# A hybrid decoder step on one core: where the convolution, its gate and the key norms of the gated DeltaNet heads are computed

## What is computed

```
conv = full[:, 0:T] * conv_w[0]
for j in range(1, G_CONV):                       # G_CONV = 4
    conv = conv + full[:, j:j + T] * conv_w[j]
q, k, v = split(silu(conv), 3)
q = l2norm(heads(q)) * HEAD_DIM ** -0.5
k = l2norm(heads(k))
beta = sigmoid(b_logit);  g = -exp(a_log) * softplus(a_logit + dt_bias)
G = cumsum(g);  decay = exp(G_i - G_j)           # inside chunks
```

## Time and profile before

| | us |
|---|---|
| median of 3 runs | 2923.39 |
| the profiled execution | 2920.07 |
| its span | 2917.9 |
| PE busy in the span | 2698.5 |
| DVE busy | 1668.2 |
| ACT busy | 947.1 |
| POOL busy | 161.5 |

### The profile page before, as it was taken

One profiled execution on the slowest core, in us unless ns is written; L12 is line 12 of the kernel. 1 busy time (PEld: TensorE's weight loads), 2 busy tenths in 40 slices (PEclk: granted clock), 3 DMA queues, 4 the chain that ended last, 5 costly groups with the idle time before them and its releaser, 6 DMA issues.

```text
span 2917.9 us, 59294 instructions
## 1 busy us (share of the span) xinstructions
PE 2698.5 (92%) x23238; PEld 2519.8 (86%) x23238; DVE 1668.2 (57%) x2503; ACT 947.1 (32%) x1694; POOL 161.5 (6%) x168
## 2 busy tenths in 40 slices
PE   8999999978887899999999999999787879999996
PEld 8999999857665789999999999988666668999996
DVE  5666337654646466663356653467456655666534
ACT  4333224332212243332233332333222223333323
POOL 1030110000000010001100001100000001000011
PEclk9999999977867999999999999999777889999998
DMA  4852334200000323222222222431000022222221
GB/s 110 106 90 88 88 93 135 59 24 5 10 8 2 94 74 90 87 87 83 79 87 86 86 83 87 130 99 39 27 1 9 10 65 59 80 86 86 88 88 56
DMA packets 380501, 201.67 MB, mean 69 GB/s; under 512 B 41461, under 2 KB 376821, under 8 KB 379528
## 3 DMA queue, kind: packets, MB, share of 16 engines
q1 hardware_dynamic: 377928, 197.46, 23.2%
q0 software_dynamic: 2400, 1.82, 1.9%
HBM read 188.07 MB, written 13.34 MB: 69 GB/s over the span
## 4 chain that ended last, share of the span: by engine, by line
PE 78%; DVE 10%; issue 5%; ACT 4%; DMA 1%; SPq 1%; DVEq 0%; POOLq 0%; ACTq 0%; POOL 0%
PE ps L683 53%; PE ps L738 24%; DVE ar L1926 3%; DVE ar L1920 2%; ACT ar L1421 2%; DVE wl L1804 1%; ACT wh L1352 1%; PE ps L1012 1%; SPq L530 1%; DVE x L1920 1%; DMA raws<-in_ffn_w_in 0%; DVE ar L1956 0%; DVE xl L1911 0%; DVE ar L1923 0%; DMA raws<-in_w_in 0%
## 5 line engine op out<-in xcount | busy, mean ns | idle before, releaser
L1804 DVE TENSOR_TENSOR wl<-raws,wh 128x1024 fp32r<-128x1024 f32 x336 | 411.3, 1225 | 662.0 <-ACT wh L1352 657.8
L683 PE MATMUL ps<-xh,wh 128*128 128x272 f32 x2880 | 604.8, 291 | 18.5 <-DVE wl L1804 16.0
L738 PE MATMUL ps<-ar 64*64 64x64 f32 (+13 forms) x5408 | 484.1, 277 | 133.7 <-ACT ar L1421 37.8
L683 PE MATMUL ps<-xh,wl 128*128 128x272 f32 x2880 | 599.8, 290 | 0.0
L683 PE MATMUL ps<-xl,wh 128*128 128x272 f32 x2880 | 598.5, 289 | 0.0
L738 PEld LDWEIGHTS ps<-ar 64*64 64x64 f32 (+6 forms) x5408 | 359.7, 162 | 233.1 <-issue 66.1
L1352 ACT ACTIVATE wh<-raws 128x1024 fp32r<-128x1024 f32 x336 | 355.1, 1058 | 407.1 <-PE ps L683 376.4
L683 PEld LDWEIGHTS ps<-xh,wh 128*128 128x128 f32 x2880 | 457.5, 190 | 21.6 <-DVE wl L1804 18.0
L683 PEld LDWEIGHTS ps<-xl,wh 128*128 128x128 f32 x2880 | 457.9, 190 | 0.0
L683 PEld LDWEIGHTS ps<-xh,wl 128*128 128x128 f32 x2880 | 457.4, 190 | 0.0
L683 PE MATMUL ps<-hh,wh 128*128 128x272 f32 x1408 | 292.2, 289 | 0.0
(11 more groups left out here) (190 smaller groups left out, 2724.0 us busy)
## 6 DMA issues: line engine op xcount, KB each, us to landing
raws<-in_ffn_w_in SPq DMA_DIRECT2D x176, 512.0 KB, 3.6
raws<-in_ffn_w_out SPq DMA_DIRECT2D x64, 512.0 KB, 4.0
raws<-in_w_in SPq DMA_DIRECT2D x42, 512.0 KB, 3.5
raws<-in_ffn_w_out SPq DMA_DIRECT2D x32, 384.0 KB, 3.4
raws<-in_w_out SPq DMA_DIRECT2D x16, 448.0 KB, 4.0
x_kept<-x SPq DMA_DIRECT2D x2, 2176.0 KB, 10.1
x<-x_kept SPq DMA_DIRECT2D x2, 2176.0 KB, 7.9
ar<-in_consts SPq DMA_DIRECT2D x2, 1337.5 KB, 6.6
```

The costliest lines, as they stand in the source:

```text
L683: ins = pe.matmul(ps[:, bank + h, 0:n1 - h * NH], w[u % 2][:, k, :], a[:, k0 + k, h * NH:n1], start=(first and k == 0 and n == 0), stop=(l ...
L738: return pe.matmul(dst, lhsT, rhs, start=start, stop=stop, **kw)
L1804: dve.tensor_tensor(wl[u % 2][:, :, :], raw[u % 2][:, :, :], wh[u % 2][:, :, :].bitcast(F32), ALU.subtract).then_inc(sem("wl_done"), 1)
```

## The change

The four taps and the silu of pairs 2 and 3 leave `prepare_gdn` of DVE and go to GpSimd, which does them in the first two periods. [...] The results stay in unused chunks of `xh` and `xl` (`over_x`), the scratch in chunks of `proj` that are no longer read. ACT's tanh of the pairs stand in the inverse of pair 0 and the preparation of pair 1, its squares in the inverse of pair 1. The gated DeltaNet preparations shrink to 26 steps: sums of squares first, then the roots (ACT copies the sums out of PSUM first), the Newton step on SBUF operands, beta, `cum`, and `dif` behind the first product steps of the recurrence; `token_major` is step 5.

```diff
-PREPARE_STEPS = (27, 27 + GATE_STEPS, 30, 30)
+PREPARE_STEPS = (27, 27 + GATE_STEPS, 26, 26)
...
+        over_x = sb("over_x", [P, 2, KC, NX])
...
+                if self.gd:
+                    self.W = [over_x[:, t, k, 0:NT] for t, k in (((0, 1), (1, 1), (0, 6)), ((1, 6), (0, 7), (1, 7)))[self.c]]
+                    self.sq = proj[:, GCH + self.c:GCH + self.c + 3:2, :]
+                    self.y = proj[:, self.c:self.c + 3:2, :]
...
+        conv_tmp = [over_x[:, 0, 0, 0:NT], over_x[:, 1, 0, 0:NT], proj[:, V_CH, :]]
+        tap_tmp = [pairs[3].W, [proj[:, GCH + 2 * j, :] for j in range(3)]]
+        CONVOLVED = lambda c, k: 45 * c + 36 + 2 * (k + 1)
```

PE, `prepare_gdn`, up to `token_major`, after:

```diff
+                    norm_sums_of(p)
+                    yield
+                    pe.wait_ge(sem("qk_out"), at(lay, "qk_out", c + 1))
+                    pe.wait_ge(sem("beta"), at(lay, "beta", 1))
+                    for h in range(2):
+                        ins = mm(ps[:, 2 + h, 0:NH], cst("sel", 8)[:, c * P:(c + 1) * P], proj[0:8, BA_CH, h * NH:(h + 1) * NH])
+                    ins.then_inc(*tick("beta_b"))
                     pe.wait_ge(sem("ge"), at(lay, "ge", c + 1))
...
                     ins.then_inc(*tick("cum"))
-                    for i in range(TILES):
...
-                    ins.then_inc(*tick("dif"))
-                    yield
                     yield
                     pe.wait_ge(sem("dec"), at(lay, "dec", 2 * q - 1))
...
                     yield
+                    pe.wait_ge(sem("kk_read"), at(lay, "kk_read", q + 1))
+                    for i in range(TILES):
...
+                    ins.then_inc(*tick("dif"))
                     yield
                     yield
                     pe.wait_ge(sem("dec"), at(lay, "dec", 2 * q))
                     pe.wait_ge(sem("dif_min"), at(lay, "dif_min", 3 * (c + 1)))
-                    pe.wait_ge(sem("qk_sq"), at(lay, "qk_sq", 2 * (c + 1)))
-                    blk_sum(U[:, 3, :], 0, "qk_sum")
-                    blk_sum(U[:, 4, :], 2, "qk_sum")
```

ACT:

```diff
+                def conv_tanh(p, k):
+                    act.wait_ge(sem("conv"), at(lay, "conv", CONVOLVED(p.c, k)))
+                    if p.c:
+                        act.wait_ge(sem("conv_s"), at(lay, "conv_s", k + 1))
+                    go(conv_tmp[k], p.W[k], ACT.Tanh, scale=0.5).then_inc(*tick("conv_t"))
...
+                def norm_roots(p):
+                    act.wait_ge(sem("qk_sum"), at(lay, "qk_sum", p.c + 1))
+                    act.wait_ge(sem("conv_s"), at(lay, "conv_s", 3 * (p.c + 1)))
+                    sums = ps[:, 3, 0:2 * NSAMP].rearrange("p (k n) -> p k n", k=2)
+                    go(p.sq[:, :, 0:SEQ], ps[:, 1:3, :])
+                    go(p.sq[:, :, SEQ:NT], sums)
+                    go(p.y[:, :, SEQ:NT], sums, ACT.Ln, bias=eps_l2).then_inc(*tick("a_ln"))
+                    go(p.y[:, :, 0:SEQ], ps[:, 1:3, :], ACT.Ln, bias=eps_l2).then_inc(*tick("qk_out"))
...
+                    go(p.y, p.y, ACT.Exp, scale=-0.5).then_inc(*tick("rs_exp"))
...
+                    if q == 1:
+                        for k in range(3):
+                            conv_tanh(pairs[3], k)
...
+                        if q == 0 and li == 1:
+                            for k in range(3):
+                                conv_tanh(pairs[2], k)
+                        if q == 1 and li == 2:
+                            act.wait_ge(sem("conv"), at(lay, "conv", 2 * 42 + 3))
+                            qk_squares(pairs[2])
+                        if q == 1 and li == 3:
+                            qk_squares(pairs[3])
```

DVE, `prepare_gdn`, after (the four calls of `tap`, the three silu operations and the later Newton step are gone from it):

```diff
+                    newton(p.y, p.sq, L2_EPS, p.sq, "rs_exp", "d_seq", q + 1)
+                    stt(U[:, K_, :], p.W[1], 0.5, p.y[:, 1, :], ALU.mult, ALU.mult).then_inc(*tick("d_seq"))
+                    dve.wait_ge(sem("beta_b"), at(lay, "beta_b", c + 1))
+                    stt(halves(U[:, BV, :]), halves(p.W[2]), 0.5, bank2(2), ALU.mult, ALU.mult).then_inc(*tick("d_seq"))
+                    dve.wait_ge(sem("d_seq"), last(lay, "d_seq"))
+                    stt(halves(U[:, NBK, :]), halves(U[:, K_, :]), -1.0, bank2(2), ALU.mult, ALU.mult).then_inc(*tick("kk_read"))
+                    stt(U[:, Q_, :], p.W[0], 0.5 * HD ** -0.5, p.y[:, 0, :], ALU.mult, ALU.mult).then_inc(*tick("d_seq"))
```

GpSimd, new, in front of its wait for `head_l` 4:

```diff
+                def tap(p, s):
+                    for j in range(3):
+                        ch = 2 * j + p.c
+                        wt = par("conv_w")[:, (3 - s) * 6 + ch:(3 - s) * 6 + ch + 1]
+                        dst = tap_tmp[p.c][j] if s else p.W[j]
+                        pool.tensor_scalar(dst[:, s:SEQ], proj[:, GCH + ch, 0:SEQ - s], wt, None, ALU.mult).then_inc(*tick("conv"))
+                        pool.tensor_scalar(by_samples(dst), xe[:, ch, :, 3 - s:7 - s], wt, None, ALU.mult).then_inc(*tick("conv"))
+                    conv_done()
+                    for j in range(3 if s else 0):
+                        dst, add = p.W[j], tap_tmp[p.c][j]
+                        pool.tensor_tensor(dst[:, s:SEQ], dst[:, s:SEQ], add[:, s:SEQ], ALU.add).then_inc(*tick("conv"))
+                        pool.tensor_tensor(dst[:, SEQ:NT], dst[:, SEQ:NT], add[:, SEQ:NT], ALU.add).then_inc(*tick("conv"))
...
+                        pool.tensor_tensor(conv_tmp[j], conv_tmp[j], p.W[j], ALU.mult).then_inc(*tick("conv"))
+                    conv_done()
+                    for j in range(3):
+                        pool.tensor_tensor(p.W[j], p.W[j], conv_tmp[j], ALU.add).then_inc(*tick("conv_s"))
...
+                pool.wait_ge(sem("xe"), at(lay, "xe", 1))
+                pool.sem_inc(passed, 1)
+                for s in range(4):
+                    tap(pairs[2], s)
...
+                for s in range(4):
+                    tap(pairs[3], s)
+                    if s == 1:
+                        conv_silu(pairs[2])
+                conv_silu(pairs[3])
```

More of the change, by code:

```diff
@@ L908, in banks_free, with norm_sums_of @@
                         pe.sem_inc(passed, 1)
+                def norm_sums_of(p):
+                    pe.wait_ge(sem("qk_sq"), at(lay, "qk_sq", 2 * (p.c + 1)))
+                    pe.sem_inc(passed, 1)
+                    for k in range(2):
+                        mm(ps[:, 1 + k, :], cst("blk"), p.sq[:, k, 0:SEQ])
+                    for k in range(2):
+                        ins = mm(ps[:, 3, k * NSAMP:(k + 1) * NSAMP], cst("blk"), p.sq[:, k, SEQ:NT])
+                    ins.then_inc(*tick("qk_sum"))
                 def prepare_rwkv(p):
@@ L983, in prepare_gdn @@
                     yield
+                    pe.wait_ge(sem("kk_read"), at(lay, "kk_read", q + 1))
+                    for i in range(TILES):
+                        for hp in range(2):
+                            g = ge[:, i, hp * HD:hp * HD + 1].broadcast_to([P, P])
+                            dst = ps[:, 2 + i // 2, (i % 2 * 2 + hp) * P:(i % 2 * 2 + hp + 1) * P]
+                            mm(dst, g, cst("gd")[:, 0:P], stop=False)
+                            ins = mm(dst, cst("neg_incl"), g, start=False)
+                    ins.then_inc(*tick("dif"))
                     yield
@@ L1582, in prepare_gdn @@
                     act.wait_ge(sem("state_out"), at(lay, "state_out", 64 * (q - 1)))
+                    norm_roots(p)
+                    yield
                     yield
@@ L1586, in prepare_gdn @@
                        ps[:, 0:2, :].rearrange("p a n -> p (a n)").rearrange("p (i k n) -> p k i n", i=TILES, k=2), ACT.Exp).then_inc(*tick("dec"))
-                    for n in range(2):
-                        act.wait_ge(sem("dif_min"), at(lay, "dif_min", 3 * c + n + 1))
-                        go(gram[:, 4 * n:4 * n + 4, 2 * P:3 * P], gram[:, 4 * n:4 * n + 4, 2 * P:3 * P], ACT.Exp).then_inc(*tick("dif_e"))
                     yield
@@ L1640, in inverse @@
                     yield
-                    for _ in range(1, len(LEVELS)):
+                    for li in range(1, len(LEVELS)):
+                        if q == 0 and li == 1:
[6 more added lines that the diff above has]
+                            qk_squares(pairs[3])
                         yield
@@ L2206, in prepare_gdn @@
                     dve.sem_inc(*tick("ge"))
-                    dve.wait_ge(sem("xe"), at(lay, "xe", 1))
-                    for k in range(3):
-                        tap(k)
-                        dve.wait_ge(sem("d_seq"), last(lay, "d_seq"))
+                    newton(p.y, p.sq, L2_EPS, p.sq, "rs_exp", "d_seq", q + 1)
+                    stt(U[:, K_, :], p.W[1], 0.5, p.y[:, 1, :], ALU.mult, ALU.mult).then_inc(*tick("d_seq"))
+                    dve.wait_ge(sem("beta_b"), at(lay, "beta_b", c + 1))
```

134 lines of the change are left out of this document (54 added, 80 removed).

## The result

The changed kernel took 2874.53 us in the median of its runs beside 2924.65 for the kernel before: a ratio of 0.984, 95% interval 0.9805 to 0.9875. Two later comparisons of the same two kernels gave 0.9838 (0.9811 to 0.9864) and 0.983 (0.9799 to 0.986). Its profiled execution took 2875.93 us, with a span of 2874.1 against 2917.9.

A forecast was written before the change was run, and what follows sets the result against it. PE was taken as the bound, busy 2698.5 of 2917.9 us. Gain -32.8 plus cover 21 gave -11.8: 2908.3 from the profiled 2920.07, 2911.6 from the median; forecast's own range 2901 to 2921, overall range 2885 to 2940.

The forecast's parts named there:

- The holes: Third and fourth periods up to token_major's first transposes: 24.4 and 23.0 us, instead of 35.9 and 34.4.
- The two moved finish steps: Finish steps pushed behind token_major in the third and fourth periods: charged 4.3 and 2.2 us.
- The gain: Third and fourth periods, shorter holes less moved finish steps: net 7.2 and 9.2 us, 16.4 a layer, 32.8 in all.
- rival (a): First two periods: cover nearly free, DVE seldom meets POOL, 2898; with PE's clock rising earlier, 2890; chance 0.24.
- The cover: Work added in the first two periods, mainly POOL slowing DVE: cost 10.5 us a layer, 21 in all.
- The price of a meeting: First two periods: a two-input SBUF operation of DVE loses 0.5 us to POOL's operations.
- my sign: Expected in the changed profile: DVE's two-input operations between 620 and 700 above 1.1 us, where they were 0.72.
- POOL's prices: First two periods: tensor_scalar 0.96 us, add 1.36, contention 15; POOL done at 699, before ACT asks at 706.6.
- rival (c): Second period: ACT waits for POOL's late taps; decides above 1.25 us per tensor_scalar; 2936 or 2955 us; chance 0.17.

The follow-up runs named there:

- e5_conv_only_delay: Kernel before with only convolution and silu moved to the first two periods, plus six idle DVE operations in each hole: 2921.73 us, 1.0014 to the kernel before.
- e1_cover: Kernel before plus POOL's and ACT's added work of the first two periods as idle work that nothing reads: 2922.28 us, ratio 1.0009.
- part one alone: Kernel before with convolution and silu moved to the first two periods, norms left late with 30 steps: 2921.95 us, ratio 1.0014.

## Why the prediction was wrong

**The holes: right.** 23.5 and 22.1 us stand against my 24.4 and 23.0. The chain went as I wrote it down; ACT's part of it in the fourth period:

```profile
875.50 1.14 ACT L1436 ACTIVATE ar<-ps 128x1024 f32<-128x1024 f32 x2 [1.00 <-DVE xl L1960]
...
880.62 1.11 ACT L1436 ACTIVATE ar<-ar 128x1088 f32<-128x1088 f32 x1
```

From the head's end at 875.2 to the end of the exponential are 6.5 us; I had 6.3. DVE's Newton step ended at 10.5 for my 10.3.

**The two moved finish steps: about right.** Charged 4.3 and 2.2; the second layer's rest of the third period grew by 5.4 (57.9 to 63.3) and the fourth's by 1.4 (42.8 to 44.2). With four more steps the third period only shifts this work, as I assumed, but the fourth loses 4.3 us, which I had not seen.

**The gain: mis-sized, because PE's clock was put at nothing.** "Net 7.2 and 9.2 us" took the rest as the same but for the moved steps. Measured are 14.5 and 5.8 in the third periods and 10.9 and 11.0 in the fourth, 42 in all for my 33. The first layer had 65.3 us at 0.74 in its rest (I cited that row, and used it only in rival (a), as 8 us); after the change it is 63.2 or 63.3 at 0.86 or 0.87, in both layers and in all three profiles of the changed kernel. Over the four periods of both layers the matmuls took 10 to 19 us less for a term that my sum does not have. Why the clock comes so is open; e5_conv_only_delay shows that it hangs on the hole before.

**The cover: the step that failed.** "Cost 10.5 a layer, 21 in all" measured 2.6 us in all (-4 to +9). The price of a meeting was right: the operations that were slowed lost 0.46 us each, for my 0.5. Wrong was that each of 14 operations on the chain of waits meets POOL and passes its delay on. In a first period 9 or 10 of DVE's 76 instructions were slowed, by 3.6 and 6.0 us in sum. Of DVE's 17 us over both layers 6.2 came out as idle time of PE, 3.1 a layer for my 10.5 (my sign, 1.1 us for a two-input operation, was 0.87), and PE's granted clock (0.75, 0.79, 0.70, 0.77 in the first two periods of the layers, against 0.71, 0.77, 0.71, 0.77 before) took 6.5 us off its matmuls. Rival (a) had this outcome, DVE seldom meeting POOL and a clock that rises earlier, at 2898 or 2890, with a cover of 8 us and a clock worth 8, both too careful.

**The sum put right.** 42 us for the third and fourth periods less 2.6 for the cover are 39 us, where the two first profiles show 41, the second ones (676.4 and 628.0) 48, and the medians 50. The 2 to 11 us that remain are not accounted for: the interval of e1_cover alone is 13 us wide, and the profiles of one kernel differ by 2.8 and 4.7 us in these periods.

**POOL's prices: wrong, and harmless by 4 us.** I put a `tensor_scalar` at 0.96 us, between memset and add; it took 1.57, above my threshold of 1.25 for rival (c); the 0.5 to 0.8 that stands beside it as an estimate was further off. "POOL is late" still did not come true: the adds took 1.08 to 1.26 in place of 1.36, contention cost POOL 8.6 us where I had put 15 (its operations up to 706.0 took 85.3 us in sum in the first layer, 76.7 by the least of each shape), and ACT itself came at 709.9, not 706.6. That POOL came in time was luck: by my own sum, with its 15 us of contention, 1.57 gives 714, 7 us late, and would have eaten the gain; errors in four terms cancelled. Fifteen more additions brought rival (c)'s loss: 45 us back.

**How DVE and POOL share.** "SBUF — State Buffer" of the Trainium skill (section "Who interferes with whom") has DVE's two-input operations and POOL's exclude each other. The longer DVE operations here agree, 867 against 735 ns in the mean. But 36 of the 63 that overlapped one of POOL's in the first two periods of e1_cover took no longer than alone, and 30 of these had started while POOL's was running, most of them in its last part. Two in its second layer, of which the first lay whole inside POOL's operation:

```profile
2055.55 1.56 POOL L2582 TENSOR_SCALAR over_x<-ar 128x512 f32<-128x512 f32 x1
...
2056.10 1.49 DVE L1957 SCALAR_TENSOR_TENSOR ar<-ar 128x544 f32<-128x544 f32 x2
```

The two take 1.49 us in the kernel before too (0.73 each and the gap between them), and 1.56 is POOL's usual length; the profile's spans on POOL are rough. So the rule agrees in part, and counting its price on every operation of the chain was my error. The row that I priced it by was misread too: the operation at 1341.54 (1.72 us) is one of 24 of line 1911 that all took 1.66 to 1.78, and the 0.78 belongs to the line's other 24, of another form, which took up to 1.95.

## What to carry to other kernels

Price contention by how many operations really meet, in the engine's busy time, and then ask what of it reaches the engine that bounds the stage: 8.6 us a layer on DVE were 3.1 us of idle time on PE. Split a gain into idle time and busy time of that engine before explaining it: PE's idle time agreed within 2 us between profiles of one kernel, its busy time moved by 5 with the clock. Where PE is the bound and its clock alternates between two levels, the stretch behind a hole must be read together with the hole: shortening the hole by 4 us cost 7.5 behind it, and 12 us gained up to 14.5. A part of a change that shows nothing by itself may still be needed: part one alone gained nothing (1.0014), and with the second it was 0.984.

## What was not expected of the hardware

- A POOL `tensor_scalar` with a scalar per partition took 1.57 us for 512 columns and 0.36 for 32 where nothing held it up; an add of 510 columns 1.08 and of 32 columns 0.24. With one full input less it was the dearer one.
- Three one-input `tensor_scalar` of DVE (128 by 544) took 3.84 us beside POOL's silu and 1.26 alone. Contention is not limited to DVE's operations with two inputs.
- PE's granted clock: the same 30 matmuls took 4.15 us at the upper level (2.4 GHz) and 6.59 at the lower (1.2 GHz), after holes in which PE did the same work and that differ by one gap of 4 us, the longer hole being followed by the upper level. The whole kernel took the same time with such a gap in all four holes and without, 2921.73 and 2921.95 us.
- The same period of the same kernel comes out in a few lengths (second period 91.8 or 97.5 us; rest of the third 57.8, 62.2 or 65.3), each with its mean clock.
